# Overflow slots of a mixture of experts as further rounds of the experts' own loop

## The reference

```python
g_top = top-1 of 4 groups;  e_idx = top-2 of the 8 experts in that group
combine = one_hot(group) * (weights of the two experts) * p_top      # (tokens, 32)
h = silu(einsum("nd,edf->nef", uf, w_gate)) * einsum("nd,edf->nef", uf, w_up)   # D_EXPERT = 256
h = h * combine[:, :, None]
y = einsum("nef,efd->nd", h, w_down)
```

## Time and profile before

| | us |
|---|---|
| timed runs, median of 3 (lowest, highest) | 1755.57 (1753.15, 1760.03) |
| the profiled execution, its time | 1752.1 |
| the profiled execution, its span (first to last instruction) | 1750.3 |
| TensorE busy in the span | 1496.6 |
| VectorE, ScalarE, GpSimd busy | 746.7, 509.8, 169.3 |
| mean granted TensorE clock | 0.916 |

### The profile page before, as it was taken

How to read it: one execution, slowest core, us unless ns; L and a number is a source line. 1 busy time by engine, 2 the same in 40 slices (tenths; PEclk the granted TensorE clock), 3 DMA queues, 4 the chain that set the end, 5 groups by cost and what they waited for, 6 DMA issues and landing times. The chain is left out here.

```text
span 1750.3 us, 20250 instructions
## 1 busy us (share of the span) xinstructions
PE 1496.6 (86%) x7317; PEld 772.8 (44%) x7331; DVE 746.7 (43%) x1900; ACT 509.8 (29%) x958; POOL 169.3 (10%) x226
## 2 busy tenths in 40 slices
PE   3999879999999999799759987999519999999940
PEld 3455324545544444366436655455204444444430
DVE  4002625687869787567735543122421111111105
ACT  3113422535457741366523321000101111111100
POOL 0001000000000000000033320000051111110004
PEclk9899659999999999899869998999759999999975
DMA  7722221001040000200098993882128999999638
GB/s 210 205 117 96 81 73 25 1 1 25 1 145 22 24 25 24 109 1 1 4 358 343 377 374 113 281 281 80 37 46 259 352 357 358 360 354 351 239 108 306
DMA packets 152649, 285.37 MB, mean 163 GB/s; under 512 B 36777, under 2 KB 106057, under 8 KB 144201
## 3 DMA queue, kind: packets, MB, share of 16 engines
q1 hardware_dynamic: 127600, 164.35, 28.8%
q0 software_dynamic: 21264, 106.88, 16.6%
q10 hardware_dynamic: 3696, 12.98, 1.9%
HBM read 243.04 MB, written 46.26 MB: 165 GB/s over the span
## 5 line engine op out<-in xcount | busy, mean ns | idle before, releaser
L450 PE MATMUL x_psZ<-w,uT 128*128 128x512 f32 (+1 forms) x864 | 383.9, 599 | 6.3 <-PEq L64 6.3
L450 PEld LDWEIGHTS x_psZ<-w,uT 128*128 128x128 f32 (+1 forms) x864 | 156.8, 186 | 204.3 <-issue 203.3
L1902 PE MATMUL e_psG<-e_wgu,e_xT 128*96 128x512 f32 x512 | 227.0, 596 | 1.4 <-DVE e_xT L1957 1.4
L1968 DVE TENSOR_TENSOR e_h<-e_gate,e_psG 96x256 f32<-96x256 f32 x32 | 13.4, 418 | 310.8 <-ACT e_gate L1935 310.8
L1902 PEld LDWEIGHTS e_psG<-e_wgu,e_xT 128*96 128x96 f32 x512 | 81.5, 164 | 122.4 <-issue 122.4
L1552 PE MATMUL o_ps<-o_w,k_mixT 128*128 128x512 f32 (+1 forms) x288 | 129.1, 602 | 6.3 <-DMA o_w<-in_w_out 6.1
L1890 PE MATMUL e_psY<-e_wd,e_hT 128*96 128x512 f32 x256 | 115.2, 593 | 1.7 <-ACT e_hT L1941 1.7
L1070 DVE TENSOR_SCALAR_CACHE_REDUCE x_junk<-sc,x_mid 128x384 bf16<-128x384 f32 (+3 forms) x128 | 109.2, 909 | 1.1
L1324 PE MATMUL s_psK<-k_identity,s_ring 128*128 128x128 f32 x512 | 80.0, 302 | 34.4 <-DMA s_ring<-in_cache_k,k_quarter_id 14.8
L1324 PEld LDWEIGHTS s_psK<-k_identity,s_ring 128*128 128x128 f32 x512 | 60.3, 151 | 63.9 <-issue 23.4
L1552 PEld LDWEIGHTS o_ps<-o_w,k_mixT 128*128 128x128 f32 (+1 forms) x288 | 52.5, 187 | 70.9 <-issue 62.8
(11 more groups left out here) (334 smaller groups left out, 2026.2 us busy)
## 6 DMA issues: line engine op xcount, KB each, us to landing
e_wgu<-in_w_gate SPq DMA_DIRECT2D x32, 1024.0 KB, 10.5
e_wgu<-in_w_up SPq DMA_DIRECT2D x32, 1024.0 KB, 13.8
e_wd<-in_w_down SPq DMA_DIRECT2D x32, 1024.0 KB, 8.7
w<-in_w_in SPq DMA_DIRECT2D x6, 2048.0 KB, 9.5
y_rows<-e_y ACTq DMA_DIRECT2D x32, 384.0 KB, 7.2
y_rows<-sc SPq DMA_DIRECT2D x16, 512.0 KB, 15.3
skew<-bias_rows SPq DMA_DIRECT2D x8, 576.0 KB
n_x<-in_x_prompt SPq DMA_DIRECT2D x8, 512.0 KB, 4.1
```

Of the source, the lines that this page charges most:

```text
L450: mm = nc.tensor.matmul(psZ[u % 2][:rows_of(i), :], A["uT"][:, k, cols_of(i)], w[:, c, k, :], start=(k == 0), stop=(k == KD - 1))
L1902: mm = nc.tensor.matmul(psG[:CAP, b, :], xT[:, b, k, :], wgu[:, j, k, :], start=(k == 0), stop=(k == KD - 1))
```

## The change

The overflow stage goes. The number of slots is rounded up to whole rounds (`ROUNDS` = 14, `SLOTS` = 56 for 54), and the experts' loop ends at a round that the router leaves in `M["last_round"]`: 7, and one more for every begun group of four overflow slots. `M["expert_of"]` names the expert of each of the 56 slots: its own number below 32, the overflow's expert from there on, 31 for those beyond the need. SP reads it before each slot's loads. Round 7 is no longer written out, so its engines' code is that of the loop; TensorE's last slot turns one more slot's rows, for which GpSimd does one more gather. A slot that fills up the last round has a list of zeros, so its tokens are 96 times token 0, and its result is stored where nobody reads.

```diff
-SLOTS = NE + OVER
+RING = 4
+ROUNDS = -(-(NE + OVER) // RING)
+SLOTS = ROUNDS * RING
...
@@ route, VectorE @@
-            link(V.tensor_copy(M["over_count"][:, :], over[:, 1, NE - 1:NE]))
-            for v in range(OVER):
-                link(V.tensor_scalar(prod[:, 0, :], over[:, 1, :], float(v), None, ALU.is_le, ALU.add, accum_out=ovx[:, v:v + 1]))
-            link(V.tensor_scalar(ovx[:, :], ovx[:, :], float(NE - 1), None, ALU.min))
-            V.tensor_copy(M["over_expert"][:, :], ovx[:, :])
+            MORE = SLOTS - NE
+            link(V.tensor_tensor(extra[:, :, :], over[:, 1, :].unsqueeze(1).to_broadcast([P, MORE, NE]),
+                                 A["expert_id"][:, :MORE].unsqueeze(2).to_broadcast([P, MORE, NE]), ALU.is_le))
+            link(V.tensor_reduce(ovx[:, :], extra[:, :, :], AX_X, ALU.add))
+            link(V.tensor_scalar(M["expert_of"][:, NE:], ovx[:, :], float(NE - 1), None, ALU.min))
+            link(V.tensor_copy(M["expert_of"][:, :NE], A["expert_id"][:, :]))
+            link(V.tensor_scalar(ovx[:, :MORE // RING], A["expert_id"][:, :MORE // RING], float(RING), None, ALU.mult))
+            link(V.tensor_scalar(ovx[:, MORE // RING:2 * (MORE // RING)], ovx[:, :MORE // RING], over[:, 1, NE - 1:NE], None, ALU.is_lt, ALU.add,
+                                 accum_out=left[:, :]))
+            V.tensor_scalar(M["last_round"][:, :], left[:, :], float(NE // RING - 1), None, ALU.add)
@@ experts: rounds, every engine @@
             for j in range(RING):
                 body(0, j)
-            with engine.Fori(1, NE // RING - 1) as it:
+            last = engine.value_load(M["last_round"][0:1, 0:1], min_val=NE // RING - 1, max_val=ROUNDS - 1)
+            with engine.Fori(1, last + 1) as it:
                 for j in range(RING):
                     body(it, j)
-            for j in range(RING):
-                body(NE // RING - 1, j)
+            return last
@@ experts, SP @@
                 e = it * RING + j
+                expert = sp.value_load(M["expert_of"][0:1, bass.ds(e, 1)], min_val=0, max_val=NE - 1)
                 sp.wait_ge(g_ready, e - (RING - 1))
-                load_gate_up(sp, S, E, e, j)
+                load_gate_up(sp, S, E, expert, j)
                 sp.wait_ge(y_ready, e - (RING - 1))
-                load_down(sp, S, E, e, j)
+                load_down(sp, S, E, expert, j)
@@ experts, GpSimd @@
+            last = rounds(pool, body)
+
+            pool.wait_ge(x_turned, last * RING + 1)
+            pool.wait_ge(x_loaded[0], last * 16 + 16)
+            pool.sem_inc(gathers, 1)
+            gather(0, slice(0, 1), last * RING + RING)
@@ experts, TensorE @@
-                if not (isinstance(it, int) and e == NE - 1):
-                    turn(it, j + 1)
+                turn(it, j + 1)
...
-            rounds(pe, body)
-            down(NE // RING - 1, RING - 1)
+            last = rounds(pe, body)
+            down(last, RING - 1)
@@ experts, ScalarE @@
-            rounds(act, body)
-            store(NE // RING - 1, RING - 1)
+            last = rounds(act, body)
+            store(last, RING - 1)
             for b in range(2):
-                act.wait_ge(y_stored[b], 16 * NE // 2)
+                act.wait_ge(y_stored[b], last * (RING // 2) * 16 + RING // 2 * 16)
+            act.sem_inc(y_taken, 1)
@@ experts, VectorE @@
-                if not (isinstance(it, int) and e == NE - 1):
-                    take_tokens(it, j + 1)
+                take_tokens(it, j + 1)
...
-def overflow_experts(nc, S, A, M):
...
@@ build @@
-        M["over_count"] = sb(top, "m_over_count", [P, 1], I32)
-        M["over_expert"] = sb(top, "m_over_expert", [P, OVER], I32)
+        M["last_round"] = sb(top, "m_last_round", [P, 1], I32)
+        M["expert_of"] = sb(top, "m_expert_of", [P, SLOTS], I32)
...
-        overflow_experts(nc, S, A, M)
         combine(nc, S, M)
```

More of the change, by code:

```diff
@@ L38 @@
 OVER = 2 * TOK // CAP
-SLOTS = NE + OVER
+RING = 4
+ROUNDS = -(-(NE + OVER) // RING)
+SLOTS = ROUNDS * RING
 MULTIPLES = TOK // CAP + 1
-RING = 4
 BISECT = 32
@@ L1658, in route @@
         cmp_t = sb("cmp_t", [P, NE, MULTIPLES])
-        ovx = sb("ovx", [P, OVER])
+        extra, ovx, left = sb("extra", [P, SLOTS - NE, NE]), sb("ovx", [P, SLOTS - NE]), sb("left", [P, 1])
         zeros = sb("zeros", [P, -(-SLOTS * CAP // P)], U32)
@@ L1853, in _, with gather @@
         def _(pool):
+            def gather(j, column, e):
+                nc.gpsimd.tensor_copy(ids[:, j:j + 1], M["token"][:, column]).then_inc(ids_ready, 1)
+                pool.wait_ge(ids_ready, e + 1)
+                pool.sem_inc(gathers, 1)
+                pool.indirect_dma_start(xg[:, j, :], None, S["xn"], bass.IndirectOffsetOnAxis(ap=ids[:, j:j + 1], axis=0)
+                                        ).then_inc(x_loaded[j], 16)
             def body(it, j):
@@ L1858, in body @@
                     pool.wait_ge(x_loaded[j], it * 16)
[L1859 to L1864, removed]
+                gather(j, bass.ds(e, 1), e)
+            last = rounds(pool, body)
+            pool.wait_ge(x_turned, last * RING + 1)
+            pool.wait_ge(x_loaded[0], last * 16 + 16)
+            pool.sem_inc(gathers, 1)
+            gather(0, slice(0, 1), last * RING + RING)
         @block.tensor
@@ L1968, in body @@
                 nc.vector.tensor_tensor(h[:, b, :], gate[:, b, :], psG[:CAP, b, DE:], ALU.mult).then_inc(h_ready, 1)
-                if not (isinstance(it, int) and e == NE - 1):
-                    take_tokens(it, j + 1)
+                take_tokens(it, j + 1)
             take_tokens(0, 0)
             rounds(dve, body)
-def overflow_experts(nc, S, A, M):
[L1977 to L2064, removed]
-                                            A["ln2_gT"][:, 4 * half:4 * half + 4].unsqueeze(2).to_broadcast([P, 4, CAP]),
-                                            ALU.mult).then_inc(xT_ready, 1)
-                dve.wait_ge(gate_ready, s + 1)
-                nc.vector.tensor_tensor(hT[:, :, :], gate[:, :, :], psG[:, K2 * CAP:2 * K2 * CAP].rearrange("p (f c) -> p f c", f=K2),
-                                        ALU.mult).then_inc(h_ready, 1)
```

## The result

| us | before | after |
|---|---|---|
| median (lowest to highest) | 1756.51 (1753.15 to 1760.03) | 1726.07 (1724.70 to 1729.52) |
| the profiled execution, its span | 1752.1, 1750.3 | 1725.3, 1723.5 |

The account below looks back on a forecast made before the run. TensorE was taken to pace the experts, with the overflow stage an exposed chain behind them. +44.53 + 0.66 - 33.6 + 0.15 + 0.15 = +11.9 us on 1755.57 gave 1767 us, range 1760 to 1773 (8 in 10).

Parts of the forecast that it names:

- What the change asks for: Experts' loop: one overflow slot makes last_round 8, so nine rounds of four, 36 slots, only one new slot with tokens.
- Added on TensorE: Experts' loop: four more slots at 11.133 us, full price even if empty, +44.53 us; turning an unused slot, +0.66.
- Rival B: Experts' rounds become DMA-paced: 1807 us if 32 slots slow, 1772 if only the last four do; chance 0.05.
- Removed behind the experts: Last down product's end to the combine's first gather: 40.28 us shrinks to a 6.7 us tail, so 33.6 us go.
- The loop's end: Last expert slot: turning a slot nobody uses, +0.66 us; final store's address from a register, +0.15; last hT wait unchanged.
- Reads of registers: Queues' reads of last_round and SP's reads of expert numbers: hidden under queued work and waits, 0 us.
- rival D: TensorE's queue: register read (1.3 us) or two back branches (1.1 each) exposed, 1768 to 1769 us; chance 0.10 alone.
- The router: Router: 22 small reductions go, seven operations come, hidden by 13 us of cover before the Pool's scatters end; 0 us.
- The +0.15 for two more columns of the list: Token table grows from 54 to 56 columns, so its exposed read of 4.2 us grows by 0.15 us.
- Rival C: Experts' loop doesn't take the overflow slot, last_round comes out as 7: 1723 us; chance 0.02.
- Rival A: Removed overflow stage is dearer in ordinary runs than the profiled one: 1764 us, or 1760 at most; chance 0.17.

Follow-up runs that it names:

- Experiment 1: The kernel before with 2 added to the router's count of overflow slots: 1785.12 us (one run), against 1757.83 for the kernel before beside it.
- experiment 3: The changed kernel with last_round one higher, so nine rounds and 36 slots, four with lists of zeros: 1770.84 us, ratio to before 1.0086.
- experiment 6: The changed kernel with the router's comparison of 128 x 768 elements on VectorE done nine times over: 1724.46 us (one run).

## Why the prediction was wrong, step by step

- **"What the change asks for" failed, in its first sentence.** "One overflow slot means last_round = 7 + 1 = 8" rested on "its loop ran exactly once here". That row was right and the reading of it wrong: a pass of this loop proves a count of zero or one. Nothing that was read of that trace tells the two apart. But the earlier trace rows had the warning, six comparisons for the six passes of the fixed loop and so none ahead of the first; with the test at the end a single pass says nothing of a need, and the number of pairs of the fullest expert (87 of 96 places) had to be asked of the reference. Experiment 1 settles it; without that term the sum is 0.66 - 33.6 + 0.3 = -32.6, against -29 measured and -26.8 in the traces (-30.7 without the stages ahead of the router).
- **Added on TensorE**: 44.53 us did not come, since no slot did. As a price it was right: 44.8 us in the time and 4 x 11.135 in the trace of experiment 3, where the four slots added have nothing in them. Rival B (DMA pace) fell with it.
- **Removed behind the experts**: 33.6 forecast, 33.61 measured, with a tail of 6.67 for 6.7. Both of its parts came out: the barrier 4.5 us behind the last down product (1680.0) and the gather 2.1 us behind that, with the two clearings between.
- **The loop's end** was mis-sized: +0.66 + 0.15 forecast, +2.66 measured. The turning was right. Missed was that hT comes 0.30 us later in code of the loop than in a round written out: ScalarE's copy of hT starts 1.61 us behind its copy of the results, against 1.47, with a store between whose address is in a register now, and two hand-offs are 0.09 and 0.07 us longer. The loop's rounds of the kernel before have the same 1.61 us (1585.31 to 1586.92). The lower clock in the last down product, 1.70 us, was missed as well.
- **Reads of registers**: no cost, as forecast. TensorE read the number under its own queue, and slot 4's product followed without a gap:

```profile
L1835 PEldq TENSOR_LOAD <-m_last_round x1: 492/492/492, 1353.0 to 1353.0; - x1
...
L1836 PEldq COMPARE_BRANCH  x7: 76/208/240, 1397.6 to 1664.9; - x7
```
```profile
1352.57 3.60 PE L1906 MATMUL e_psY<-e_wd,e_hT 128*96 128x512 f32 x8
...
1356.18 7.03 PE L1918 MATMUL e_psG<-e_wgu,e_xT 128*96 128x512 f32 x16
```

  The slots before and behind it are 11.13 us, so rival D fell too. SP's reads of an expert's number, 28 and not 32, as the weights of the first four slots are loaded earlier, took 268 ns each (median) and delayed no load that mattered.
- **The router** was not free: +0.85 us. The cover of 13 us held for VectorE's own end (its seven operations took 3.0 us in place of 5.6), but the wide one lengthened a scatter on the Pool, which is the exposed chain (0.53 us; experiment 6). Another 0.26 us came between the first copy of token ids and the first turning, and 0.07 between the read of the list and that copy; their cause is not traced. The +0.15 for two more columns of the list did not show: its read landed after 4.6 us in both kernels, and the 4.2 us that the prediction took for this landing were SP's wait behind it.
- **Rival C** gave 1723 us, near the measured 1726, for a wrong reason: it supposed that the changed loop would miss a needed slot. That it ends 3 us from the measured time is luck. It got 0.02 because "the old loop ran once on the same number" was counted against it, the same misreading a second time. Rival A (a dearer stage in ordinary runs) is not needed: the removed stretch is 33.61 us in the traces, and the times differ by 29.

## What to carry to other kernels

Before a count is read off how often a loop's body ran, look where its comparison stands: with the test at the end, zero looks like one, and a stage "for the rare case" is paid in every execution, here 33.6 us of 1756. A further round of a busy pipeline cost its plain rate, 11.13 us a slot, with tokens or without, as long as the weights kept up (16 us a slot with 86 places), whereas a stage of its own cost 27 to 34 us for each further slot. So with this ring of four, folding in wins at none (29 us) and at two slots (14 us at 96 places with empty slots, 27 at 80 with real ones, by the clock of the old stage). It loses at one: 13 us at 96 places, by experiment 3 against the kernel before, whose one pass for none stands for one slot, and 17 us at 86, where DMA sets the pace.

## What was not expected of the hardware

- The last down product of the experts took 5.37 us behind a wait of 2.03 us in all three traces with eight rounds (mean clock 0.68 where it was read), and 3.65 to 3.67 us in all three with nine rounds and a wait of 2.03 or 1.95.
- The same isolated stage ran its products at a mean clock of 0.82 with 96 places in a slot and 0.53 with 80, which made a pass 27.18 or 33.64 us long.
- A VectorE operation on two operands of 128 x 768 elements lengthened the Pool's issue of a scatter from 0.97 to 1.50 and 1.68 us while it ran.
- Slots of 86 rows instead of 96 cost 192 us: stores with two packets besides the data instead of sixteen, gathers of 704 packets instead of 112, and 111 us of waits for weights on TensorE. With 80 rows stores and gathers had sixteen packets besides the rows again, and gathers landed after 7.4 us.
